# A layout change for the tokens of an expert loop: contiguous rows of 256 high and 256 low numbers

## The reference

```python
def one_block(args):
    hb, eb, gb = args                      # tokens, picked experts, gates
    a = jnp.einsum('td,tkd->tk', hb, peer_u[eb], preferred_element_type=jnp.float32)
    a = jax.nn.gelu(a, approximate=False)
    return jnp.einsum('tk,tkd->td', (gb * a).astype(hb.dtype), peer_v[eb])
```

## Time and profile before

| what | before |
|---|---|
| median of 3 runs | 958.64 us (958.21 to 959.58) |
| profiled execution, time | 957.38 us |
| profiled execution, span of the core | 955.6 us |
| TensorE busy | 948.3 us, 99% of the span |
| VectorE busy | 753.0 us, 79% |
| ScalarE busy | 468.7 us, 49% |
| GpSimd busy | 209.6 us, 22% |
| up matmuls, 512 columns (line 1976) | 728 |
| up matmuls, 256 columns (line 1979) | 728 |
| down matmuls, 512 columns (line 1996) | 1536 |
| data moved | 174.72 MB, 183 GB/s on average |

### The profile page before, as it was taken

One profiled execution on the slowest core, in us unless ns is written; L12 is line 12 of the kernel. 1 busy time (PEld: TensorE's weight loads), 2 busy tenths in 40 slices (PEclk: granted clock), 3 DMA queues, 4 the chain that ended last, 5 costly groups with the idle time before them and its releaser, 6 DMA issues.

```text
span 955.6 us, 16376 instructions
## 1 busy us (share of the span) xinstructions
PE 948.3 (99%) x5324; PEld 829.7 (87%) x5324; DVE 753.0 (79%) x1453; ACT 468.7 (49%) x849; POOL 209.6 (22%) x249
## 2 busy tenths in 40 slices
PE   9999999999999999999999999999999999999998
PEld 9998899998999987888888888888888888888887
DVE  6899759998999988888677777767767767767766
ACT  6576554423899963344344344344344344344342
POOL 3075138886777720000000000000000000000000
PEclk9999999999999999999999999999999999999999
DMA  9544138726544468776665666666666666665664
GB/s 296 150 133 133 45 115 283 206 78 211 148 140 130 138 204 243 239 239 231 199 192 183 196 188 186 196 188 186 194 187 190 195 186 188 194 188 188 192 188 147
DMA packets 73593, 174.72 MB, mean 183 GB/s; under 512 B 6208, under 2 KB 39104, under 8 KB 73296
## 3 DMA queue, kind: packets, MB, share of 16 engines
q1 hardware_dynamic: 73120, 172.02, 58.2%
q0 software_dynamic: 288, 2.10, 1.1%
q10 hardware_dynamic: 144, 0.08, 0.0%
HBM read 165.26 MB, written 6.82 MB: 180 GB/s over the span
## 4 chain that ended last, share of the span: by engine, by line
PE 93%; ACT 3%; DVE 2%; DMA 2%; issue 0%; SPq 0%; POOL 0%; POOLq 0%; DVEq 0%; ACTq 0%
PE psum L1996 35%; PE psum L1976 17%; PE psum L1861 11%; PE psum L1979 9%; PE psum L1561 5%; PE psum L1830 4%; PE psum L1939 3%; PE psum L1577 2%; DMA rr<-big 1%; PE psum L1618 1%; PE psum L1739 1%; PE psum L1822 1%; PE psum L1855 1%; ACT rr L788 1%; DMA gel<-up_kept 1%; PE psum L1605 0%
## 5 line engine op out<-in xcount | busy, mean ns | idle before, releaser
L1996 PE MATMUL psum<-rr 128*128 128x512 f32 x1536 | 366.4, 391 | 0.2 <-DVE rr L1311 0.2
L1996 PEld LDWEIGHTS psum<-rr 128*128 128x128 f32 x1536 | 287.5, 188 | 60.4 <-DVE rr L1311 0.8
L1976 PE MATMUL psum<-h_all,rr 128*128 128x512 f32 x728 | 260.6, 392 | 0.0
L815 ACT ACTIVATE rr<-raw 128x1024 fp32r<-128x1024 f32 x94 | 99.7, 1061 | 295.7 <-PE psum L1996 294.5
L1279 DVE TENSOR_TENSOR rr<-raw,rr 128x1024 fp32r<-128x1024 f32 x94 | 115.2, 1225 | 125.2 <-ACT rr L815 125.2
L1979 PE MATMUL psum<-h_all,rr 128*128 128x256 f32 x728 | 188.7, 280 | 0.0
L1976 PEld LDWEIGHTS psum<-h_all,rr 128*128 128x128 f32 x728 | 136.6, 188 | 26.9
L1979 PEld LDWEIGHTS psum<-h_all,rr 128*128 128x128 f32 x728 | 136.7, 188 | 7.2
L1861 PE MATMUL psum<-t32s,raw 128*128 128x256 f32 x576 | 131.4, 379 | 0.0
L1861 PEld LDWEIGHTS psum<-t32s,raw 128*128 128x128 f32 x576 | 106.3, 190 | 12.7
L1193 DVE TENSOR_TENSOR rr<-raw,rr 128x1024 fp32r<-128x1024 f32 x90 | 109.8, 1220 | 1.4 <-ACT rr L704 1.4
(11 more groups left out here) (215 smaller groups left out, 1125.6 us busy)
## 6 DMA issues: line engine op xcount, KB each, us to landing
raw<-in_peer_v_dram SPq DMA_DIRECT2D x128, 512.0 KB, 3.5
raw<-in_peer_u_dram SPq DMA_DIRECT2D x127, 512.0 KB, 3.7
big<-in_w_in_dram SPq DMA_DIRECT2D x10, 1024.0 KB, 6.0
big<-in_peer_wq_dram SPq DMA_DIRECT2D x8, 1024.0 KB, 6.6
up_kept<-gel SPq DMA_DIRECT2D x36, 128.0 KB, 3.8
gel<-up_kept SPq DMA_DIRECT2D x34, 128.0 KB, 3.7
big<-in_w_out_dram SPq DMA_DIRECT2D x4, 1024.0 KB, 5.2
rr<-big POOLq DMA_DIRECT2D x2, 1024.0 KB, 9.8
```

What stands on the lines that cost most here:

```text
L815: act.activation(v_sp[s][:, 0, :], v_raw[s], ACT.Copy).then_inc(v_hi, 1)
L1976: return pe.matmul(both, ut[s][:, 0, k, :], ht[:, :, k, :], start=(k == 0), stop=(k == DK - 1))
L1996: i = pe.matmul(psum[:, 4 + 2 * t + n, :], g_sp[:, s, x, t * P:(t + 1) * P], v_sp[s][:, y, n * 512:(n + 1) * 512], start=(first and m == 0 ...
```

## The change

The tokens' parts for the expert loop, and the gates' high part, are placed differently inside `h_all`. The projections and query products still use the old views `hm` and `ht`. From the copy at line 754 on, the first 4096 numbers of `h_all` are seen as chunk, part, token (`hs`, 8 x 2 x 256), so that the 256 high numbers of a chunk and its 256 low numbers lie behind one another, and each row of 512 starts on a multiple of 2048 bytes. The last 256 numbers (`p_high`) take the gates' high part in one run instead of 16 pieces of 16. The wide matmul of `up` reads one run of 512 numbers instead of two runs of 256. The number of instructions, their shapes, the waits and the transfers stay.

```diff
         h_all = sb("h_all", [P, 2, DK, T], F32R)
         hm, ht = h_all[:, :, :, 0:META], h_all[:, :, :, META:T]
+        h_flat = h_all[:, :, :, :].rearrange("p a k t -> p (a k t)")
+        hs = h_flat[:, 0:2 * DK * SEQ].rearrange("p (k a t) -> p a k t", a=2, k=DK)
+        p_high = h_flat[:, 2 * DK * SEQ:2 * DK * SEQ + SEQ]
...
         def p_hi(tok, n):
-            return hm[:, tok // P, tok % P // META, tok % META:tok % META + n]
+            return p_high[:, tok:tok + n]
...
-            act.activation(ht[:, 0], t32s, ACT.Copy).then_inc(a_hi, 1)
+            act.activation(hs[:, 0], t32s, ACT.Copy).then_inc(a_hi, 1)
...
-            act.activation(hm, psum[:, 7, 0:SEQ].rearrange("p (a k m) -> p a k m", a=2, k=DK), ACT.Copy).then_inc(pk_ev, 1)
+            act.activation(p_high, psum[:, 7, 0:SEQ], ACT.Copy).then_inc(pk_ev, 1)
...
-                    dve.tensor_tensor(picks[:, 2, :].rearrange("p (a k m) -> p a k m", a=2, k=DK),
-                                      psum[:, 7, 0:SEQ].rearrange("p (a k m) -> p a k m", a=2, k=DK), f(hm), ALU.subtract)\
-                       .then_inc(d_plo, 1)
+                    dve.tensor_tensor(picks[:, 2, :], psum[:, 7, 0:SEQ], f(p_high), ALU.subtract).then_inc(d_plo, 1)
...
-                pool.tensor_tensor(ht[:, 1, ks, :], t32s[:, ks, :], f(ht[:, 0, ks, :]), ALU.subtract).then_inc(p_hlo, 1)
+                pool.tensor_tensor(hs[:, 1, ks, :], t32s[:, ks, :], f(hs[:, 0, ks, :]), ALU.subtract).then_inc(p_hlo, 1)
...
-                product(psum[:, 2 * s, 0:SEQ], lambda a, k: ut[s][:, a, k, :], lambda b, k: ht[:, b, k, :], a_done)
+                product(psum[:, 2 * s, 0:SEQ], lambda a, k: ut[s][:, a, k, :], lambda b, k: hs[:, b, k, :], a_done)
...
-                    return pe.matmul(both, ut[s][:, 0, k, :], ht[:, :, k, :], start=(k == 0), stop=(k == DK - 1))
+                    return pe.matmul(both, ut[s][:, 0, k, :], hs[:, :, k, :], start=(k == 0), stop=(k == DK - 1))
...
-                    pe.matmul(both[:, 0, :], ut[s][:, 1, k, :], ht[:, 0, k, :], start=False, stop=False)
+                    pe.matmul(both[:, 0, :], ut[s][:, 1, k, :], hs[:, 0, k, :], start=False, stop=False)
```

## The result

The change made the kernel slower. The median went from 958.12 us (956.39 to 959.58) to 961.16 us (959.69 to 962.23), a ratio of 1.0032 with a 95% interval of 1.0026 to 1.0039: 3.0 us more, where 5.1 less were forecast. The profiled execution took 960.89 us, 959.1 of them span.

The account below looks back on a forecast made before the run. It took TensorE's distances between matmul starts as the bound. Savings of 5.0 us in the loop's up parts and 0.1 in the first up product gave 958.64 - 5.1 = 953.5 us; the range ran from 951.0 to 959.5.

Parts of the forecast that it names:

- What bounds the kernel: Expert loop: TensorE, busy 99% of the span, is the bound; time is the sum of distances between matmul starts.
- The yardstick: Down part's aligned 512-column products, 0.2267 us apart; at that pace an up pair would cost 0.2267 + 0.1133 = 0.34.
- The fourth pair at 0.34: Up part: the fourth row, first on a multiple of 256 bytes, takes 0.34 exactly and so is at the floor.
- The extra belongs to the weight load beside it: Narrow streams: the extra 0.005 us comes from full 128-column weight loads, since 16-column weights run at 0.1139.
- The down part as a stream without loss: Expert loop's down part: a full weight load beside a 512-column stream can cost nothing when both are aligned.
- rival A: Whole path locks: up part at the floor and down part's entry cost gone, 6.9 us less, 951.7; chance 0.12.
- Part 1: Expert loop's up part: contiguous, aligned rows make every pair cost 0.34, saving 0.055 a block, 5.0 us over 91 blocks.
- Part 2: First up product, 24 narrow matmuls: from 0.1186 to between 0.1186 and 0.1139 each, taken as 0.1 us saved.
- Part 3: Entry cost of the down part, 0.02 a block: may vanish for 0 to 1.8 us, taken as 0.
- Parts 4 to 6: Copy and subtractions: 0; gates' high part: 0.02 us at most, once; VectorE's slack of 0.52 shrinks by at most 0.06.
- C: Rival: nothing moves; if only 64-byte lines matter, the alternation of widths itself sets the distances; 958.6 us, chance 0.27.
- D: Rival: slower, aligned reads clash in step in each pair; 9 us at worst, 963.2 with half the pairs; chance 0.13.

## Why the prediction was wrong

**What bounds the kernel:** right. The time is the sum of the distances between matmul starts, and a kernel of those alone gives them.

**The yardstick:** here it failed. The down part shows an aligned stream of 512-column products at 0.2267, and the step went from there to "a pair would cost 0.34" for an aligned alternation of two widths. The narrow term, 0.1133, was half of the wide one, and no row had it with full weights: the prediction's own rows had 0.1186 there. Aligned narrow products take 0.1200, and the aligned alternation 0.347 a pair, the mean of before, or 0.353. The loop took the dear pace, hence +3.0; at the cheap one, in which TensorE alone ran the first block of after, the up part took 2.77 against 2.78 before, so even there nothing near the forecast was to be had. The 0.34 exists, but at another place (U high 64 bytes earlier).

**The fourth pair at 0.34:** a reading of one pair, though the right one: none of the first six is shorter in any of the 82 whole blocks between 448 and 900 us (0.340 on average, and the third pair 0.340 too). It was taken as proof that a row on a multiple of 256 bytes is at the floor. After the change all rows are there, and only the first pair shows 0.34. A pair's length depends also on what ran before it: 0.347 or 0.353 at the same addresses (lines 555 and 545).

**"The extra belongs to the weight load beside it":** right in that moving U high alone takes the aligned block from 5.55 to 5.47; wrong in the size argument, since 16-column weights leave it at 5.57 and 5.55. The 0.1139 of the earlier trace rows holds for the narrow width alone.

**The down part as a stream without loss** (also what stood for rival A): only the last products of a block are. Where down parts follow one another before the loop, the mean is (80.94 - 0.39) / 352 = 0.2288, not 0.2267, by this row of before, all of it aligned (two waits in it cost under 0.2 us together):

```profile
359.28 80.94 PE L1996 MATMUL psum<-rr 128*128 128x512 f32 x353 [0.19 <-DVE rr L1311]
```

**Part 1,** priced at -5.0, measured +3.0 (91 x 0.033). **Part 2,** -0.1: the first up product went from 0.1186 to (3.03 - 0.28) / 23 = 0.1196, some 0.02 us more, by this row of TensorE's order of time:

```profile
345.84 3.03 PE L1562 MATMUL psum<-h_all,rr 128*128 128x256 f32 x24
```

**Part 3,** the entry cost of the down part, taken as 0: its first six products take 1.54 instead of 1.55, so it stayed. That it can vanish through the up part's state was in the text, and in the kernel with U high 64 earlier it does vanish. **Parts 4 to 6** held, but for the 0.02 of part 5: the counts are 728 and 728, the copies keep their lengths (1.92 us for the high part, 1.28 for each subtraction, 0.41 for the gates' high part), no wait was added, and VectorE's low part ends at 709.42 + 1.22 = 710.64, 0.56 us ahead of the weight load at 711.20. With blocks of 5.467 that slack was 0.47, within what part 6 allowed.

**The rivals.** C, the alternation itself costs, held for the aligned places and not in general: with U high 64 earlier its pairs take 0.340. And multiples of 64 bytes do differ (U high 128 and 192 later, 5.57 and 5.47), as do steps under 64 (tokens 16 and 20 later, 5.50 and 5.59). D named the sign, the stretch and the test: a mean pair over 0.3475, now 0.351, all along the up part. It was given 0.13 and 963.2 us; the price was half of the way to the dearest pair seen, and 0.0041 a pair came instead of 0.00625. Against D stood that down parts "leave the clash after five matmuls"; the aligned alternation, once in its dear pace, does not leave it in 24 pairs (line 545). That this is a clash of reads, met again and again, was not shown. The evidence for D was in the same rows as that for the forecast: a pair of 0.34 between pairs of 0.35 and 0.36 says that places matter by 0.02, not which place is good.

**The plain fp32 products** of the earlier trace rows, 27.20 / 126 = 0.2159 apart, say nothing of the pace of 512 columns. `early_part` writes 288 products (36 blocks of 8) and the trace has 576 records of line 1861, so one plain product takes two records, 0.432 us; one of fp32r with 256 columns is one record, 0.1186. The records of line 1861 have 256 columns, by this row of before:

```profile
208.69 27.58 PE L1861 MATMUL psum<-t32s,raw 128*128 128x256 f32 x127
```

**Open:** why a given distance is cheap. The runs show that tokens 256 bytes on cost the same, that 4-byte steps count, that a common shift of 64 bytes does not, and that there is more than one steady pace for one set of addresses. No rule was found from which the 5.467 could be worked out instead of measured.

## What to carry to other kernels

Where TensorE is the bound and its products are fp32r, the byte distance between streamed rows and weights was worth -1% to +2% of a block here (5.47 to 5.62 against 5.52), and alignment was no virtue in itself (5.55 aligned, 5.47 at the best place): a yardstick taken from a stream of one width did not carry to the mix of widths (0.340 a pair forecast, 0.351 measured). Scan the distances with TensorE alone, in the real order of products and through several blocks: such a kernel gave the whole kernel's block to 0.01 us for all five placements that were run both ways. Scan in single steps and in combination, since here a good place was lost by 4 bytes (5.47 to 5.54 and 5.57) and two gains together were a loss (5.47 and 5.50 alone, 5.59 together, 5.55 with neither). Then write the offset inside a tile, since a padding tile of 16 bytes moved its neighbour by 32.

## What the runs showed of the hardware

- The closest fp32r products with full weights are 0.2264 (down part with U high 64 bytes earlier) to 0.2269 (aligned, TensorE alone) apart at 512 columns and 0.1133 at 256 (weights 64 bytes off); the plain fp32 products of the earlier trace rows are recorded as two products of 256 columns each (576 records for 36 blocks of 8), 0.2159 apart.
- A product's weight load runs beside the product ahead of it: in the kernel after, line 1980's load of 0.19 us and line 1977's product of 0.39 us both start at 711.42.
- An aligned alternation of the two, full weights, takes 0.347 or 0.353 a pair; with U's high part 64 bytes earlier it takes 0.340.
- The weights' place changes the pace of the stream: 0.2269 or 0.2333 wide, 0.1197 or 0.1137 narrow, and the good places differ for the two widths (weights 0, 16 and 240 bytes later for 512 columns, 64 for 256).
- One alternation at one set of addresses runs at 0.347 or 0.353 a pair, through the last 12 of its 24 pairs, by what came before.
- Weights of 16 columns make wide products dearer (0.2314) than full ones at a good place (0.2269).
